# Two-layer hybrid decoder trunk on one Trainium2 core: gate rows folded by transfers instead of TensorE, padding cleared later, a pair's last scores moved

## The reference

```python
for i in range(DEPTH):                       # 2
    h = rmsnorm(x, norm1[i])
    if i % 2 == 0:
        mix, xq = mlstm_mixer(h, ...)        # p = h @ w_in; q,k: causal conv + silu; 8 gate columns
    else:
        mix, xq = diff_attention(h, ...)     # 12 heads of 64 as 6 pairs, rope, 4 query blocks of 128
    xo = memory_cross_attention(xq, mem, ...)
    x = x + concatenate([mix, xo]) @ w_out[i]
    h = rmsnorm(x, norm2[i])
    gu = h @ w_gate_up[i]
    x = x + (silu(gu[..., :2816]) * gu[..., 2816:]) @ w_down[i]

# in mlstm_mixer: gates are 8 of the columns of p
gates = p[..., 4*768 : 4*768+8] + gate_b
i_pre, f_pre = gates[..., :4], gates[..., 4:]
log_f = log_sigmoid(f_pre);  b = cumsum(log_f);  a running maximum of i_pre - b gives the stabiliser
```

## Time and profile before

| | |
|---|---|
| median of 3 runs | 1235.92 us (1235.68 to 1236.24) |
| the profiled execution's own time | 1235.87 us |
| its span from first to last instruction | 1234.0 us |
| PE busy | 1227.9 us, 99% of the span |
| POOL busy | 844.9 us, 68% |
| DVE busy | 519.2 us, 42% |
| ACT busy | 360.7 us, 29% |
| granted clock of PE | 1.000 in the mean |

### The profile page before, as it was taken

One profiled execution on the slowest core, in us unless ns is written; L12 is line 12 of the kernel. 1 busy time (PEld: TensorE's weight loads), 2 busy tenths in 40 slices (PEclk: granted clock), 3 DMA queues, 4 the chain that ended last, 5 costly groups with the idle time before them and its releaser, 6 DMA issues.

```text
span 1234.0 us, 16220 instructions
## 1 busy us (share of the span) xinstructions
PE 1227.9 (99%) x5848; PEld 1002.9 (81%) x5848; DVE 519.2 (42%) x795; ACT 360.7 (29%) x716; POOL 844.9 (68%) x1029
## 2 busy tenths in 40 slices
PE   9999999999999999999999999999999999999998
PEld 7888877788888888888888777778888888888887
DVE  6954434644222233112345888884423113221331
ACT  6523456633220011001141666655322001100110
POOL 7998433567777777777776444536678777777775
PEclk9999999999999999999999999999999999999999
DMA  7234211123232222222243222222323223323223
GB/s 274 96 122 146 69 53 46 57 86 99 97 102 95 92 102 91 96 102 98 77 132 101 71 69 71 70 69 68 101 86 102 103 85 102 102 87 101 96 72 105
DMA packets 35067, 116.99 MB, mean 95 GB/s; under 512 B 4417, under 2 KB 4930, under 8 KB 34886
## 3 DMA queue, kind: packets, MB, share of 16 engines
q1 hardware_dynamic: 33416, 112.82, 27.4%
q10 hardware_dynamic: 1598, 3.51, 1.1%
HBM read 111.05 MB, written 2.11 MB: 92 GB/s over the span
## 4 chain that ended last, share of the span: by engine, by line
PE 97%; DVE 1%; ACT 1%; issue 0%; DMA 0%; POOL 0%; ACTq 0%; SPq 0%; POOLq 0%
PE PS L1551 95%; PE PS L1952 1%; DVE nmB L1455 0%; DVE Al L1279 0%; PE PS L1795 0%; DMA w_raw<-in_wt_dram 0%; PE PS L1980 0%; PE PS L1921 0%; PE PS L1913 0%; PE PS L1619 0%; PE PS L1905 0%; DVE PS L1453 0%; DVE PB L1467 0%; ACT tmp L800 0%; ACT tmp L808 0%
## 5 line engine op out<-in xcount | busy, mean ns | idle before, releaser
L573 POOL TENSOR_TENSOR w_lo<-w_raw,w_hi 128x256 fp32r<-128x256 f32 (+1 forms) x800 | 617.5, 803 | 17.0
L568 POOL TENSOR_SCALAR w_hi<-w_raw 128x1024 fp32r<-128x1024 f32 (+2 forms) x204 | 214.7, 1052 | 356.8 <-PE PS L1551 356.7
L1551 PE MATMUL PS<-Hh,w_hi 128*128 128x512 f32 x1072 | 428.2, 399 | 0.0
L1551 PE MATMUL PS<-Hl,w_hi 128*128 128x512 f32 x1072 | 417.9, 390 | 0.3 <-DVE Hl L1059 0.3
L1551 PE MATMUL PS<-Hh,w_lo 128*128 128x512 f32 x1072 | 418.0, 390 | 0.0
L1551 PEld LDWEIGHTS PS<-Hh,w_hi 128*128 128x128 f32 x1072 | 201.3, 188 | 47.7 <-issue 8.1
L1551 PEld LDWEIGHTS PS<-Hh,w_lo 128*128 128x128 f32 x1072 | 201.2, 188 | 42.9
L1551 PEld LDWEIGHTS PS<-Hl,w_hi 128*128 128x128 f32 x1072 | 201.5, 188 | 40.4 <-issue 1.0
L1551 PE MATMUL PS<-Ah,w_hi 128*128 128x512 f32 (+1 forms) x544 | 207.9, 382 | 0.1
L1551 PE MATMUL PS<-Ah,w_lo 128*128 128x512 f32 (+1 forms) x544 | 205.0, 377 | 0.0
L1551 PE MATMUL PS<-Al,w_hi 128*128 128x512 f32 (+1 forms) x544 | 204.9, 377 | 0.0
(11 more groups left out here) (263 smaller groups left out, 993.1 us busy)
## 6 DMA issues: line engine op xcount, KB each, us to landing
w_raw<-in_wt_dram SPq DMA_DIRECT2D x181, 512.0 KB, 3.3
w_raw<-in_wt_dram SPq DMA_DIRECT2D x16, 384.0 KB, 3.0
w_raw<-in_wt_dram SPq DMA_DIRECT2D x8, 448.0 KB, 3.1
QKR<-QKP ACTq DMA_DIRECT2D x24, 128.0 KB, 4.3
xT<-in_x_t_dram SPq DMA_DIRECT2D x8, 256.0 KB, 5.6
out_dram<-xT SPq DMA_DIRECT2D x8, 256.0 KB, 2.0
mT<-in_mem_t_dram SPq DMA_DIRECT2D x1, 1024.0 KB, 10.2
cn<-in_constants_dram SPq DMA_DIRECT2D x1, 580.5 KB, 7.8
```

What stands on the lines that cost most here:

```text
L568: nc.gpsimd.tensor_scalar(w_hi[:, sl, 0:nk], w_raw[:, raw, 0:nk], 0.0, 1.0, ALU.add, ALU.mult).then_inc(w_round, 1)
L573: lo = nc.gpsimd.tensor_tensor(w_lo[:, sl, w], w_raw[:, raw, w], w_hi[:, sl, w].bitcast(F32), ALU.subtract)
L1551: return nc.tensor.matmul(out_, a, b, start=start, stop=stop)
```

## The change

The two selector matmuls on PE go away. In their place ACT issues three transfers inside SBUF, behind the first conv tap (`first_tap(0)`): rows 4 to 7 of `tmp[6]` to `tmp[0]`, rows 8 to 11 to `tmp[7]`, rows 12 to 15 to `tmp[1]`, each 4 x 512 (8 KB). DVE waits for all three behind `mem_lo(0)` and makes two additions of 4 x 512. ACT and DVE read f and i from SBUF instead of PSUM. The two clearing memsets of DVE move from ahead of `v_raw(0)` to behind `v_raw(2)`. In layer 1, `b_s(c, 3)` and `b_t(c, 1)` move one block later for pair 0, `b_s(5, 3)` moves behind the sixth row of its output tile, `c_hi(x)` moves ahead of `b_exp(c, 2)` on ACT, and `c_lo(x)` ahead of `b_max(c, 3)` on DVE.

```diff
@@ ACT
             first_tap(0)
+            act.wait_ge(g_free, 1)
+            for row, dst in ((1, tmp[0]), (2, tmp[7]), (3, tmp[1])):
+                act.dma_start(dst[0:MH, 0:SEQ], tmp[6][row * MH:(row + 1) * MH, 0:SEQ]).then_inc(gsel_done, 16)
             act.wait_ge(mss_done, 1)
...
-            act.wait_ge(gsel_done, 1)
-            link(nc.scalar.activation(tmp[0][0:MH, 0:SEQ], PS[0:MH, 3], ACT.Identity, bias=gb[:, 1:2]))
+            act.wait_ge(g_free, 2)
+            link(nc.scalar.activation(tmp[0][0:MH, 0:SEQ], tmp[0][0:MH, 0:SEQ], ACT.Identity, bias=gb[:, 1:2]))
...
                     b_sq(c + 1)
-                b_exp(c, 2)
                 if x is not None:
                     c_hi(x)
+                b_exp(c, 2)
@@ DVE
             nc.vector.tensor_reduce(rm[:], msq, AX.X, ALU.add).then_inc(msum_done, 1)
-            dve.wait_ge(msum_done, 1)
-            nc.vector.memset(KZ[0:64], 0.0)
-            nc.vector.memset(QK[64:P, MC + 1:MC + 5:3], 0.0).then_inc(k_zero, 1)
             v_raw(0)
...
             mem_lo(0)
+            dve.wait_ge(gsel_done, 48)
+            nc.vector.tensor_tensor(tmp[0][0:MH, 0:SEQ], tmp[0][0:MH, 0:SEQ], tmp[1][0:MH, 0:SEQ], ALU.add).then_inc(g_free, 1)
+            nc.vector.tensor_tensor(tmp[6][0:MH, 0:SEQ], tmp[6][0:MH, 0:SEQ], tmp[7][0:MH, 0:SEQ], ALU.add).then_inc(g_free, 1)
             conv(0)
...
+            dve.wait_ge(g_free, 3)
             link(nc.vector.memset(tmp[7][0:MH, 0:SEQ], 1.0))
...
-            link(nc.vector.scalar_tensor_tensor(a_row, PS[0:MH, 6], gb[:, 0:1], b_row, ALU.add, ALU.subtract))
+            link(nc.vector.scalar_tensor_tensor(a_row, a_row, gb[:, 0:1], b_row, ALU.add, ALU.subtract))
...
             v_raw(2)
+            dve.wait_ge(msum_done, 1)
+            nc.vector.memset(KZ[0:64], 0.0)
+            nc.vector.memset(QK[64:P, MC + 1:MC + 5:3], 0.0).then_inc(k_zero, 1)
             k_norm(0)
...
                 b_prob(c, 1)
-                b_max(c, 3)
                 if x is not None:
                     c_lo(x)
+                b_max(c, 3)
@@ PE
-            mm(PS[0:MH, 6], cn[0:16, C_GSEL:C_GSEL + MH], tmp[6][0:16, 0:SEQ])
-            mm(PS[0:MH, 3], cn[0:16, C_GSEL + MH:C_GSEL + 2 * MH], tmp[6][0:16, 0:SEQ]).then_inc(gsel_done, 1)
...
-                    if k in (0, 2):
-                        b_s(c, 2 + k // 2)
-                    if k in (5, 6):
-                        b_t(c, k - 5)
+                    if k == 0:
+                        b_s(c, 2)
+                    if k == (3 if x is None else 2):
+                        b_s(c, 3)
+                    if k == 5:
+                        b_t(c, 0)
+                    if k == (7 if x is None else 6):
+                        b_t(c, 1)
...
-                    if i in (1, 2, 4):
-                        b_s(c, i - i // 4)
+                    if i in (1, 2, 5):
+                        b_s(c, i - 2 * (i // 5))
```

## The result

The changed kernel takes 1238.72 us at the median (1236.2 to 1240.98, 18 runs) against 1235.99 (1235.66 to 1236.63, 18 runs): a ratio of 1.0020, 95% interval 1.0014 to 1.0026. That is 2.7 us slower, and outside the range I gave. The profiled execution took 1236.2 us with a span of 1234.4. It shows TensorE's clock at full speed throughout, as 4 of the 18 executions did (1236.2 to 1236.8 us); the other 14 have a mean granted clock of 0.996 to 0.999 and take 1237.7 to 1241.0. The kernel before has 1.000 in each of its 18. One more execution of it, taken beside E1 to E4, lasted 1534.2 us at a granted clock of 0.751 and is left out everywhere. So two things are to be explained: why the trace shows no gain, and what the other 2.5 us are, from the profiled execution to the median.

The account below looks back on a forecast made before the run. PE, busy in 99% of the span, was taken to bound the kernel. Selector matmuls 1.80, pair 0 0 and pair 4 0.2 sum to 2.0 us off 1235.87: 1233.9 us, range 1232.9 to 1234.9.

Parts of the forecast that it names:

- Selector matmuls: Gate stretch on PE: without them the sum over the memory tokens starts 1.80 us earlier, and that gain is kept.
- Lower parts: DVE's eight for m0, begun at 31.25 after moving the memsets, end at 35.5, a microsecond ahead of need.
- My fourth rival: Lower parts slowed by POOL to 0.92 us each end at 38.6; selector gain lost, result 1235.8 us; chance 0.05.
- Transfers hidden: The three SBUF transfers land around 33 to 34 while DVE does lower parts until 35.5, so DVE does not wait.
- Additions: DVE's two 4 x 512 additions, bounded by a 0.69 us copy, take 1.4 us; first convolution starts at 36.9.
- the margin of 1.0 us at v2: DVE empties m2 by 62.8, against 63.8 when PE's tile v2 needs it; used up if transfers land after 36.5.
- Pair 0: Layer 1: last scores' 0.66 us wait goes, but the third turn waits 0.66 us longer for ACT's copies; net 0.
- Pair 4: Layer 1: the second turn's 0.81 us goes, but later copies hold the third turn until 807.74, not 807.96; net 0.2 us.
- Pair 5: Layer 1: its wait for a turn's copy is left alone by the change; loses nothing and gains nothing.

Follow-up runs that it names:

- E1: The changed kernel with every pair move in layer 1 undone, the gate part kept: 1236.00 us, ratio 1.0000 to the kernel before.
- E4: The changed kernel without pair 0's two moves (last scores and second turn one block later): 1235.68 us, ratio 0.9999 to the kernel before.
- E9: E1 with DVE's copy of m2 put ahead of the second memory half's lower parts: 1235.22 us, ratio 0.9994 to the kernel before.
- E5: E4 with DVE's copy of m2 put ahead of the second memory half's lower parts: 1235.10 us, ratio 0.9996 to the kernel before.
- E7: E3 with one POOL split held until DVE's third probabilities of pair 0 are done: 1236.13 us, ratio 1.0001 to the kernel before.
- E3: The kernel before with only pair 0's two moves (last scores and second turn one block later): 1238.30 us, ratio 1.0015.
- E11: E5 with the last pair iteration's turns one block later, its values two, its products one: 1234.25 us, ratio 0.9989 to the kernel before.
- E2: The kernel before with all the pair moves and nothing of the gate part: 1237.23 us, ratio 1.0013.
- E10: The kernel before with the moves of `c_hi` and `c_lo` alone: 1236.05 us, ratio 1.0001.

## Why the prediction was wrong

- **Selector matmuls, 1.80 us.** Right: 1.90 at the sum.
- **Lower parts, end at 35.5.** Mis-sized. I took two at 0.92 us and six at 0.41 because POOL waits from 32.46 to 33.86. They ended at 37.05, since POOL's split of m1 then ran beside the last three. I had that split in front of me and read only one side: before, the lower parts made it long; now it makes them long. Cost: 0.74 us in m0. My fourth rival named the mechanism and gave it 0.05. It put the end at 38.6 and the time at 1235.8 us (1233.9 and the 2.1 us are 1236.0), with nothing lost further back.
- **Transfers hidden.** Right, and by more than I said: ACT's queue issued them from 26.87 on, before the first tap had started, not behind its end. No row shows when they landed; DVE had no idle time for them.
- **Additions, 1.4 us for two.** Mis-sized too: bounded by a copy that ran without POOL beside it. They took 2.3 us from the first's start to the convolution's, and POOL worked beside both. With the lower parts that makes the first convolution start at 39.3 instead of 36.9, and m2's copy end at 65.4 instead of 62.8. Of these 2.4 us at the convolution 1.5 are the lower parts' and 0.9 the additions', and only the first is more than the margin of 1.0 us at v2. The margin was real, and was overrun: the remaining 1.26 us are lost at v2. E9 and E5 show that with that copy moved they are not lost there. So the step that failed in the gate's part is the price of DVE's row: durations taken without POOL for work that ran beside it.
- **Pair 0, net 0.** The chain through maxima, exponentials and copies was as I said, to 0.1 us. What failed is "none of it depends on when PE issues the last scores". PE's earlier end of the value tile frees POOL, POOL slows the third probabilities, and the turn comes 0.78 us later. E7 shows it: hold POOL and the net is 0.
- **Pair 4, net 0.2.** Right: 0.26.
- **Pair 5, nothing.** Off by 0.2 us: the moved last scores stand 0.32 us behind the matmul ahead of them instead of 0.53.
- **The clock.** Not in the prediction in any form. It is most of the 2.7 us: the changed kernel's four executions at full clock, 1236.2 to 1236.8, are 0.2 to 0.8 us above the median of before, which leaves 1.9 to 2.5 for the clock.

So 1.8 + 0 + 0.2 = 2.0 us became 0.0 - 0.8 + 0.3 + 0.2 = -0.3, by the account of PE's starts and by the profiled executions' times alike, and -2.7 at the median with the clock. Two things remain open. One is why the clock falls in some executions behind a wait at a third turn and not behind a longer one at the second turn. E7 against E3 is the nearest to a test of the wait alone: with PE's work in the same order it goes from 1.33 to 0.66 us, and the executions below full clock from 7 to 1 of 11. E11 took pair 4's wait away and changed PE's order there too, and no run here moved one of these waits and left its length as it was. So that the wait itself is the cause is argued for pair 4, not shown. The other is why E4 had one such execution and E5, with the same pairs, four: with 11 executions each that may be chance.

## What to carry to other kernels

When work on VectorE moves, look up what GpSimd does in the new window, and do the same when TensorE moves, since its progress is what releases GpSimd; price both with durations taken beside GpSimd (here 0.47 and 0.95 us for the same instruction). Where TensorE is the bound, a gain has to pass every later hand-over: list their margins, and put a short copy that frees a PSUM bank ahead of long work that nobody waits for. Judge a wait on TensorE by where it stands and by the spread of the times, not by its length in one trace: here a loss of 0.8 us at one turn came with some 2 us more at the median through the clock.

## What the runs showed of the hardware

- A 1.33 us wait of TensorE in a stretch full of short matmuls was followed 2.2 us later by 6.8 us at a granted clock of 0.50 (1.2 GHz), which cost 3.2 us (E2); a 0.4 us wait by 3.4 us at 0.50, which cost 1.6 (E10). In neither stretch at the lower clock did PE idle. Whether it happens varies between executions of one kernel, 7 of 11 in E3.
- Two SBUF-to-SBUF additions of 4 x 512 take 1.21 us each beside POOL, although a 128 x 512 copy out of PSUM takes 0.68. No run has them without POOL beside them. A probability block (128 x 256, tensor and scalar) goes from 0.41 to 1.22 us when POOL starts together with it.
- Which of the two gives way isn't fixed, and what decides it is open. Before, POOL's split began at 33.86, 0.23 us after the first lower part, and took 3.94 us while these kept their pace. After, it began at the same 33.86, in the middle of the row of lower parts, and took 1.17 while the next one took 1.26. E5 and E11, whose programs are the same up to there, differ in the same way: DVE's instruction starts 0.03 us ahead of POOL's in both, and they take 0.67 and 1.57 us in E5, 1.62 and 1.06 in E11.
- Transfers issued from ScalarE's queue ran ahead of activations that stand before them in its program: three issues at 26.87 to 28.26, the activation ahead of them at 29.23.
